# Norm orders, three late units joined, a fourth unit behind them, and one head's output moved into the projection

## The reference

```
for i in range(DEPTH_2):                        # 2 layers
    m = mla_mixer(...) if i == 0 else gla_mixer(...)
    x = layer_norm(DN_ALPHA * x + m, ln1_g[i], ln1_b[i])
    x = layer_norm(DN_ALPHA * x + conv_ffn(x, ...), ln2_g[i], ln2_b[i])
    gate = jax.nn.sigmoid(x @ ple_w_gate[i] + ple_b_gate[i])
    x = x + gate * (p[i] @ ple_w_proj[i])

def conv_ffn(x, w_up, conv_w, conv_b, w_down):
    h = x @ w_up                                # 1024 -> 2 * 2816
    h = hp[:, 0:S] * conv_w[0] + hp[:, 1:S+1] * conv_w[1] + hp[:, 2:S+2] * conv_w[2] + conv_b
    u, g = jnp.split(h, 2, axis=-1)
    return (u * jax.nn.gelu(g)) @ w_down        # 2816 -> 1024
```

## Time and profile before

| | us |
|---|---|
| median of 3 runs | 2842.04 |
| lowest, highest | 2827.31, 2851.97 |
| the profiled execution's own time | 2839.88 |
| its span | 2837.7 |
| TensorE busy | 2741.8 (97%) |
| VectorE busy | 1670.9 (59%) |
| ScalarE busy | 1012.9 (36%) |
| GpSimd busy | 340.1 (12%) |
| TensorE in the chain that ended last | 85% |
| VectorE in that chain | 10% |

### The profile page before, as it was taken

One profiled execution on the slowest core, in us unless ns is written; L12 is line 12 of the kernel. 1 busy time (PEld: TensorE's weight loads), 2 busy tenths in 40 slices (PEclk: granted clock), 3 DMA queues, 4 the chain that ended last, 5 costly groups with the idle time before them and its releaser, 6 DMA issues.

```text
span 2837.7 us, 35499 instructions
## 1 busy us (share of the span) xinstructions
PE 2741.8 (97%) x14739; PEld 2285.3 (81%) x14739; DVE 1670.9 (59%) x2541; ACT 1012.9 (36%) x1620; POOL 340.1 (12%) x351
## 2 busy tenths in 40 slices
PE   7999999999999999999999999999999979999998
PEld 6999999876688888877676788787878758878887
DVE  6855746566456534456656567557654366764765
ACT  3222333243234222234433444334443233532434
POOL 1134413110001000020000030000410004000031
PEclk9999999999899999999999999999999979999999
DMA  4243244420033332321120222322222202233322
GB/s 139 86 121 114 94 145 139 138 68 16 30 110 102 95 106 89 91 84 49 37 79 30 75 84 91 107 89 81 91 89 76 74 15 82 82 93 100 93 78 75
DMA packets 292727, 244.03 MB, mean 86 GB/s; under 512 B 19837, under 2 KB 285575, under 8 KB 292567
## 3 DMA queue, kind: packets, MB, share of 16 engines
q1 hardware_dynamic: 282503, 226.40, 25.4%
q0 software_dynamic: 5616, 13.22, 1.5%
q10 hardware_dynamic: 4448, 2.16, 0.3%
HBM read 230.70 MB, written 13.14 MB: 86 GB/s over the span
## 4 chain that ended last, share of the span: by engine, by line
PE 85%; DVE 10%; ACT 3%; issue 1%; DMA 1%; POOL 0%; ACTq 0%; SPq 0%; DVEq 0%; POOLq 0%
PE ps L563 25%; PE ps L564 24%; PE ps L565 24%; PE ps L1768 2%; DVE ul L551 2%; PE ps L2215 2%; PE ps L2214 2%; DVE rbuf L713 1%; PE ps L698 1%; PE ps L2290 1%; ACT uh L536 1%; PE ps L1738 1%; PE ps L2979 1%; PE ps L3003 1%; PE ps L2262 1%
## 5 line engine op out<-in xcount | busy, mean ns | idle before, releaser
L551 DVE TENSOR_TENSOR ul<-raw,uh 128x1024 fp32r<-128x1024 f32 (+3 forms) x416 | 528.7, 1294 | 342.2 <-ACT uh L536 341.7
L563 PE MATMUL ps<-OH,uh 128*128 128x512 f32 (+1 forms) x1704 | 641.7, 377 | 29.3 <-DVE OL L2527 10.4
L564 PE MATMUL ps<-OL,uh 128*128 128x512 f32 (+1 forms) x1704 | 634.6, 372 | 0.0
L565 PE MATMUL ps<-OH,ul 128*128 128x512 f32 (+1 forms) x1704 | 634.4, 372 | 0.0
L536 ACT CAST uh<-raw 128x1024 fp32r<-128x1024 f32 (+3 forms) x416 | 411.6, 1025 | 171.4 <-PE ps L565 121.0
L563 PEld LDWEIGHTS ps<-OH,uh 128*128 128x128 f32 x1704 | 322.7, 189 | 94.6 <-issue 15.3
L564 PEld LDWEIGHTS ps<-OL,uh 128*128 128x128 f32 x1704 | 322.9, 189 | 55.9 <-issue 1.4
L565 PEld LDWEIGHTS ps<-OH,ul 128*128 128x128 f32 x1704 | 322.6, 189 | 55.9
L563 PE MATMUL ps<-HH,uh 128*128 128x512 f32 (+2 forms) x946 | 322.0, 340 | 11.3 <-DVE HL L2667 11.3
L563 PE MATMUL ps<-XH,uh 128*128 128x264 f32 (+1 forms) x992 | 311.9, 314 | 11.0 <-DVE ul L551 5.9
L564 PE MATMUL ps<-HL,uh 128*128 128x512 f32 (+2 forms) x946 | 321.6, 340 | 0.0
(11 more groups left out here) (425 smaller groups left out, 3790.9 us busy)
## 6 DMA issues: line engine op xcount, KB each, us to landing
raw<-in_ffn_w SPq DMA_DIRECT2D x40, 1024.0 KB, 5.1
raw<-in_ffn_w_up SPq DMA_DIRECT2D x40, 1024.0 KB, 5.0
raw<-in_ffn_w SPq DMA_DIRECT2D x32, 704.0 KB, 4.5
raw<-in_ffn_w_down SPq DMA_DIRECT2D x32, 704.0 KB, 4.5
raw<-in_w_in SPq DMA_DIRECT2D x16, 1024.0 KB, 5.4
raw<-in_gla_w_in SPq DMA_DIRECT2D x12, 1024.0 KB, 5.0
raw<-in_mla_w_o SPq DMA_DIRECT2D x8, 1024.0 KB, 5.2
raw<-in_ple_w_gate SPq DMA_DIRECT2D x8, 1024.0 KB, 6.1
```

What stands on the lines that cost most here:

```text
L551: e.tensor_tensor(l, src, h.bitcast(F32), SUB).then_inc(*s_wlo.up(("unit", u)))
L563: e.matmul(o, wh, xh, start=first, stop=False)
L564: e.matmul(o, wh, xl, start=False, stop=False)
L565: return e.matmul(o, wl, xh, start=False, stop=last)
```

## The change

The amount of computation stays the same. Only the order of work differs, and one unit more in each layer is done in two halves of the tokens, which makes 24 more matmuls of half the width.

- `staged`: after a new piece is added, every older one takes a step, also where the new one has already ended.
- `lin_start` takes `more`: one further unit (c3 of chunk 1), whose first half of the tokens lies behind the three joint units' first half. Its second half goes with theirs, piece by piece. The sums of half two lie behind piece 1 in place of piece 3.
- `lin_late` takes `between`, which head 15's output uses; the loop of heads ends one earlier.
- `ffn_*`: three `c2` units late in place of two. Both further splits come ahead of the drain of the gates. The shift for the norm comes behind the fourth unit in place of the third, and ACT and DVE split three units ahead before it.
- First norms: the root ahead of the square and the cast, the fourth unit's split between the pieces, and the statistics of half two between pieces 5 and 6.
- Second norms: two `pp` splits ahead of the root, two `pg` splits ahead of the statistics of half two, and the third ahead of the reciprocal.
- `go`: one unit further ahead at c = 2.

```diff
 def staged(pieces):
     for p in pieces:
+        older = list(steps.live)
         steps.add(p)
-        for gen in steps.live[:-1]:
+        for gen in older:
             steps.push(gen)
...
+            for name, key in zip(names, keys):
+                start(name, key)
+            for k in range(8):
+                s_lo.wait_ge(e, (tag, k, 0))
+                for u, key in us:
+                    chunk(u, key, 0, k)
+                between(k)
+            for name, key in more:
+                start(name, key)
                 for k in range(8):
+                    chunk(*us[-1], 0, k)
+            for k in range(8):
+                s_lo.wait_ge(e, (tag, k, 1))
+                for u, key in us:
+                    chunk(u, key, 1, k)
...
-        def lin_late(e, name, X, halves, xs, keys, late):
+        def lin_late(e, name, X, halves, xs, keys, late, between=None):
             for part in (range(0, kc - late), range(kc - late, kc)):
+                if part.start and between:
+                    between()
...
-                    if c or norm:
+                    if c > 1 or norm:
                         lin(e, n3, X, halves, (st, "b", c))
...
-                lin_late(e, n2, hid, halves, xs, ((st, "d", grp, 0), (st, "d", grp, 1)), 4)
+                lin_late(e, n2, hid, halves, xs, [(st, "d", grp, mm) for mm in range(late)], 4)
-                for mm in range(2, ends if grp else 8):
+                for mm in range(late, ends if grp else 8):
                     lin(e, n2, hid, halves, (st, "d", grp, mm), xs=xs)
-                    if grp and mm == 2 and shift:
+                    if grp and mm == 3 and shift:
                         shift()
...
-                feed_hi(e, n2)
+                feed_hi(e, n2, late - 1)
                 pipe.drain()
-                feed_hi(e, n2)
+                for _ in range(1, late):
+                    feed_hi(e, n2)
                 for mm in range(ends if grp else 8):
-                    if mm > 1:
+                    if mm >= late:
                         feed_hi(e, n2)
+                    if grp and mm == 2 and shift:
+                        ahead_hi(e, 3)
...
-                        lin_late(e, "mo", (OH, OL, "o1"), H2, range(8), (("mproj", 1, 0), ("mproj", 1, 1)), 2)
+                        lin_late(e, "mo", (OH, OL, "o1"), H2, range(8), (("mproj", 1, 0), ("mproj", 1, 1)), 2,
+                                 lambda: latent_output_pe(e, 15))
...
-            for i in range(19):
+            for i in range(18):
...
             pieces = [layer_piece(e, xt, i, 1, k, 0) for k in range(8)]
+            pieces[6:6] = [once(ahead_lo, e, 4), once(layer_stats_dve, e, xt, 1)]
             pieces[3:3] = [once(add, 7, 1)]
             pieces[1:1] = [once(add, 6, 1), once(ahead_lo, e, 3)]
             staged(pieces)
-            layer_stats_dve(e, xt, 1)
             inverse(e, xt, HB, hfs=(1,))
             staged([layer_piece(e, xt, i, 1, k, 1) for k in range(8)])
-            for name in ("c1", "c3", "c1"):
+            for name in ("c1", "c3", "c1", "c3"):
                 feed_lo(e, name, 0)
             ahead_lo(e, 1)
...
             for k in LAST:
                 squared(k, 0)
+            ahead_hi(e, 2)
+            layer_root_act(e, xt, 0)
             squared(5, 1)
             ahead_hi(e, 3)
-            layer_root_act(e, xt, 0)
...
-                      sums_at(e, tag, xt, 1, (3,)))
+                      sums_at(e, tag, xt, 1, (1,)), [("c3", (f"C{l}", "b", 1))])
...
+            ahead_hi(e, 6)
+            layer_root_act(e, xt, 0)
             squared(5, 1)
-            layer_root_act(e, xt, 0)
...
             for c in range(8):
                 feed_hi(e, "pp", 7 - c)
+            ahead_hi(e, 2)
             layer_high_act(e, xt, l, 2, 0, range(6, 8))
-            keep(0)
-            keep(1)
-            ahead_hi(e, 2)
+            for c in range(3):
+                keep(c)
             layer_root_act(e, xt, 1)
-            for c in range(2, 5):
-                keep(c)
+            keep(3)
             ahead_hi(e, 3)
...
+            ahead_lo(e, 2)
             layer_stats_dve(e, xt, 1)
+            ahead_lo(e, 3)
             inverse(e, xt, HB, hfs=(1,))
-            ahead_lo(e, 3)
...
-                feed_lo(e, "go")
+                feed_lo(e, "go", 2 if c == 2 else 1)
```

More of the change, by code:

```diff
@@ L884, in setup_dve, with ffn_pe @@
                     gained_dve(e, "ffn1", X1, c - 1, H[:, c - 1, :], "ffn1")
-        def ffn_pe(e, st, names, X, halves, side, param, ends, before=None, norm=None, shift=None):
+        def ffn_pe(e, st, names, X, halves, side, param, ends, before=None, norm=None, shift=None, late=2):
             n1, n3, n2 = names
@@ L919, in ffn_pe, with ffn_act @@
             side.drain()
-        def ffn_act(e, st, names, halves, gate, down, side, param, ends, before=None, norm=None, fed=0):
+        def ffn_act(e, st, names, halves, gate, down, side, param, ends, before=None, norm=None, fed=0, late=2, shift=False):
             n1, n3, n2 = names
@@ L941, in ffn_act, with ffn_dve @@
                     side.step()
-                feed_hi(e, n2)
+                feed_hi(e, n2, late - 1)
                 pipe.drain()
-                feed_hi(e, n2)
+                for _ in range(1, late):
+                    feed_hi(e, n2)
                 for mm in range(ends if grp else 8):
-                    if mm > 1:
+                    if mm >= late:
                         feed_hi(e, n2)
+                    if grp and mm == 2 and shift:
+                        ahead_hi(e, 3)
                     down(e, st, grp, mm)
                     side.step()
-        def ffn_dve(e, st, names, halves, gate, down, side, param, ends, before=None, norm=None, fed=0):
+        def ffn_dve(e, st, names, halves, gate, down, side, param, ends, before=None, norm=None, fed=0, late=2, shift=False):
             n1, n3, n2 = names
@@ L971, in ffn_dve @@
                     side.step()
-                feed_lo(e, n2)
+                feed_lo(e, n2, late - 1)
                 pipe.drain()
-                feed_lo(e, n2)
+                for _ in range(1, late):
+                    feed_lo(e, n2)
                 for mm in range(ends if grp else 8):
-                    if mm > 1:
+                    if mm >= late:
                         feed_lo(e, n2)
+                    if grp and mm == 2 and shift:
+                        ahead_lo(e, 3)
                     down(e, st, grp, mm)
@@ L2319, in latent_project_act @@
             for c in range(8):
-                feed_hi(e, "mo", 2 if half else 1)
+                if half == 0 or c:
+                    feed_hi(e, "mo", 2 if half else 1)
                 if half:
@@ L2324, in latent_project_dve @@
         def latent_project_dve(e, half):
-            if half:
-                feed_lo(e, "mo", 2)
             for c in range(5 if half else 8):
@@ L2745, in tail_pe @@
             side.add(input_pe(e, l))
-            ffn_pe(e, st, CONV, (XH2, XL2, f"x1{l}"), H2, side, none, 5, shift=lambda: layer_shift_pe(e, x2))
+            ffn_pe(e, st, CONV, (XH2, XL2, f"x1{l}"), H2, side, none, 5, shift=lambda: layer_shift_pe(e, x2),
+                   late=3)
             lin_end(e, "c2", (HH, HL, (st, "hid", 1)), HB, range(NH), [(st, "d", 1, k) for k in LAST],
@@ L2787, in tail_act @@
             side.add(input_act(e, l))
-            ffn_act(e, st, CONV, H2, conv_gate_act(l), conv_down_act(l), side, none, 5)
+            ffn_act(e, st, CONV, H2, conv_gate_act(l), conv_down_act(l), side, none, 5, late=3, shift=True)
             for mm in range(5, 8):
@@ L2846, in tail_dve @@
             side.add(input_dve(e, l))
-            ffn_dve(e, st, CONV, H2, conv_gate_dve(l), conv_down_dve(l), side, none, 5)
+            ffn_dve(e, st, CONV, H2, conv_gate_dve(l), conv_down_dve(l), side, none, 5, late=3, shift=True)
             for mm in range(5, 8):
@@ L2854, in tail_dve @@
             layer_stats_dve(e, xt, 0)
+            ahead_lo(e, 6)
             add(5, 1)
```

45 lines of the change are left out of this document (25 added, 20 removed).

## The result

Four runs of the changed kernel have a median of 2807.78 us (2806.12 to 2817.61), those of the kernel before 2841.47. The ratio is 0.9892, with a 95% interval of 0.9843 to 0.9941. Seven more runs of the same changed kernel, taken later, had a median of 2818.85 and a ratio of 0.9921 (0.9890 to 0.9951). My forecast of 2819 us, a ratio of 0.992, lies inside both intervals, 11 us above the first median and on the second. The profiled execution took 2808.3 us, with a span of 2806.5.

A forecast was written before the change was run, and what follows sets the result against it. TensorE, busy 97% of the span, bounds the kernel, so only its waits and the clock lost behind them can be won. Terms 14.7 + 2.3 + 2.4 + 1.7 + 1.1 = 22.2 us off a 2842.0 median; forecast 2819, range 2803 to 2833.

The forecast's parts named there:

- Group ends: Ends of the four hidden groups: both waits go at each, 11.3 us, plus 3.4 of clock; gain 14.7 us.
- margin of 0.3: At the group ends: the last rest ends about 1803.0, TensorE asks at 1803.3, so both waits go by 0.3 us.
- First norms: Two first norms: waits of 3.31 and 1.88 us go, smaller ones and one clock drop come; gain 2.3 us for both.
- Second norms: Before the gate units, twice: the 3.08 us wait shrinks to 1.9; gain 1.2 us each, 2.4 together.
- Head 15: Latent attention's last head: the 1.00 us wait goes, the chain to `OL` keeps part; gain 1.7 of 2.5 us.
- `go`: The `go` projection: the split goes ahead of the shift block; gain 1.1 us.
- All covers hold: Rival, chance 0.21: the replacement waits stay out everywhere; gain 38 us, 2803 us, half-way cases at 2810.
- Given back: Rival, chance 0.17: new waits bring five more clock drops of 1.7 us, 8.5 in all; gain 14, 2827 us.
- The raw tiles: Rival, chance 0.04: at group ends the third `c2` unit's load comes late and engines queue behind it; 2843 us.
- signs of being wrong: Last hidden chunks over a microsecond later than reckoned, chunk 2's wait missing, or the clock falling at new places.
- The clock: Half speed follows short waits; by the skill's longer-pause rule 3.4, 3.0 and 1.7 fall out, sum 17.5 us.
- The port: First norms: VectorE instructions contend with GpSimd's; by the skill's page 1 us more lost each, sum 20.2 us.

The follow-up runs named there:

- changed again: The changed kernel measured once more with nothing altered; 2818.85 us over seven runs, ratio 0.9921 to the kernel before.
- better: Changed kernel with chunk 2's c3 split, second norm's half-two statistics and the fourth unit's cast moved earlier; 2802.08 us, ratio 0.9871 to the kernel before.
- groups_only: The kernel before with only the group ends changed (three late units, norm's shift one unit later); 2818.75 us, ratio 0.9930.
- better3: better2 with the statistics of the first norm's half two behind the last rest of half one again; 2798.05 us, ratio 0.9827.
- better2: better with the rest of piece 1 of the first norm's half one before the scaling of piece 2; 2796.86 us, ratio 0.9832.
- before again: The kernel before measured once more with nothing changed, against itself; 2834.32 us over ten runs, ratio 0.9991.
- the small ones: The kernel before with only the parts at head 15, the second norms and `go`; 2830.04 us, ratio 0.9972.

## Why the prediction was right, step by step

- **The sum.** Predicted 22.2 us. Behind the window attention and up to the last 38 us the two first traces differ by 22.8 us (22.4 to the span's end); in changed again, with the 6.5 us of the heads' clock taken out, by 25.0. That 22.8 is so near is in part luck. The terms below came to 25.7, so I was 3.5 us short; the clock took 2.9 back, 1.5 behind the second norm of layer 1 and 1.4 in its unchanged mixer. What I didn't reckon with at all is that the two executions' unchanged parts differ, by 8.8 us ahead of the change. With them the first measurement is 1.1% faster by its ratio, past the 1% to which I had given 0.27, and the second 0.8%, where I had put 0.70. Both intervals reach across 1%.
- **Group ends**, 14.7: measured 16.4, the largest miss in size. The waits go, the clock is 1.00, and the margin of 0.3 came out as 0.12. I counted the idle times, 2.82 us an end, but they cost 3.3: the end of a 512-column matmul is shown 0.39 us after its start while its successor starts after 0.23, so idle time counted from that end misses 0.16, and the step behind a wait is about 0.1 longer. That is 0.25 a wait, 2.0 us over eight. The drop of the clock is 4.9 - 3.3 = 1.6 each, where I had 1.7.
- **First norms**, 2.3 for both: measured 3.6. The mechanism was right down to the waits: before piece 1 1.23 (I had 1.2), at pieces 5 and 6 0.39 + 1.27 (1.0), half two none (0.3). At chunk 2 0.76 in place of 1.9. The chain took the 7.2 us that I had added up, but I let it start when `lin_start` ends, with the first 512-column matmul at 1673.00. The units end piece by piece, so chunk 0's first product is ready nine half-wide matmuls earlier, and ScalarE's tap started at 1672.12:

```profile
1672.12 1.45 ACT L2657 ACTIVATE tmp<-ps,cv 128x512 f32<-128x512 f32 x2 [1.22 <-PE ps L566]
...
1678.12 2.36 DVE L552 TENSOR_TENSOR ul<-raw,uh 128x1024 fp32r<-128x1024 f32 x2 [1.53 <-ACT uh L537]
```

  The first of these two splits ends near 1679.3, and the matmul that waited starts at 1679.40, 6.4 us behind 1673.00 and not 7.4. The gain per layer, 1.8, is near the 2.0; the drop of 1.7 that I charged on one of them didn't come.
- **Second norms**, 2.4: measured 2.3, with 1.88 left at the third gate unit (I had 1.9). The profile names ScalarE's copy there, which ended at 2033.81; the split of the third gate unit ended at 2033.49, 0.36 ahead of the matmul. In better TensorE starts the gate units at 2041.10, before the last copy has ended (2041.17) and 0.39 behind the split. So I take the split for what ended the wait in both; counted from the start of `pp` it came 1.3 us sooner in better, and 0.56 was left. In layer 1 a drop of 1.5 us followed in the first trace, in both layers in the second.
- **Head 15**, 1.7: measured 2.0. **`go`**, 1.1: measured 1.4 and 1.6; the difference is the clock's, which is still low when that stage begins, and groups_only, which leaves `go` alone, shows 0.3 of it. Waits of 1.79 and 1.12 us and the 0.25 for each one fewer make 2.04 and 1.37.
- **The rivals.** "All covers hold" didn't come true: four kinds of wait stayed. "Given back" came true in part: one such drop in the first trace, two in the second, of the five. The raw tiles didn't show. Of my signs of being wrong, one came: the clock fell at a new place, in layer 1's gate units.
- **The clock.** I wrote that half speed followed where no wait was over 1.62 us. That is so at the group ends; the first window of the earlier trace rows lies behind the wait of 3.31. By the Trainium skill's "TensorE: Matmul & The Clock Gate" (Why this matters for your kernels) that wait is itself a longer pause, so the norms' 3.0 stand by it too, and the estimate from it is 22.2 - 3.4 + 1.7 = 20.5, not 17.5.
- **The port.** The loss on VectorE came, and was larger than the 1 us that I had put on it by its rule (the Trainium skill, "SBUF — State Buffer", Who interferes with whom). With half two's statistics early, GpSimd's subtractions for half two run beside half one's last scalings and rests. First the changed kernel, then, as the last row, three rests of the kernel before with GpSimd idle:

```profile
1652.37 7.10 POOL L2492 TENSOR_TENSOR H<-H,xtmp 128x256 f32<-128x256 f32 x8 [4.22 <-DVE xtmp L2537]
...
1653.59 1.83 DVE L2550 SCALAR_TENSOR_TENSOR H<-H,cv,rbuf 128x256 f32<-128x256 f32 x2
1655.35 1.82 DVE L2556 SCALAR_TENSOR_TENSOR OL<-H,cv,OH 128x256 fp32r<-128x256 f32 x2
...
1662.35 1.26 DVE L2527 SCALAR_TENSOR_TENSOR OL<-H,cv,OH 128x256 fp32r<-128x256 f32 x3
```

  That is 0.9 us each against 0.4. The 16 scalings and rests of half one took 11.4 us in place of 8.1, those of half two 6.8 in place of 8.3, 1.7 us more for VectorE in each first norm. How much of it reached TensorE no run separates; each layer's gain of 1.8 is only 0.2 under my 2.0. In better3, with these statistics behind half one again, half one's 16 took 9.4, and the wait at its end, 1.28 us in better2, was gone.

## What to carry to other kernels

Price a wait of a pipelined engine by the distance between the starts around it, less one normal step, and not by its idle time. Then compare two executions stage by stage from anchors in unchanged code: over a quarter of the profiled gain here lay ahead of the change. And when the engine that is waited for is the bound of a stretch, adding work to cover a wait can cost more than the cover, as the fourth unit did until its cast came in time for VectorE and chunk 2's split came sooner. Count the instructions of VectorE that a new order puts beside GpSimd as well: here they took twice as long.

## What I had not expected of the hardware

The granted clock's answer to a short wait depends on more than the wait. Waits of 1.64 and 1.20 us at the same place in the same instruction stream came with 0, 1.6 and 2.6 us of loss in three kernels, the waits of 3.32 and 1.88 us by 1.4 us more in one kernel than in another, and in the changed kernel 1.88 by a drop in layer 1 but not in layer 0. For the kernel before this repeats: before again agrees with it in every stage of both layers within 0.1 us, though its execution was 11 us ahead. For the changed kernel it doesn't: behind the second norm of layer 0 the same wait of 1.9 us brought no drop in the first trace and one of 1.5 us in the second. In groups_only 6.9 of the 16.4 us were given back at places that it never touched. With one profile each that can be the edit's doing or the execution's. In the same way the parts measured alone, behind the window attention, up to the last 38 us and without the heads' 6.5, make 10.4 us for the groups, 1.1 for the norms and 5.2 for the small ones, less than the 22.8 of all together. What decides where a drop comes stays open.
